# SSD groups 1 to 3: a chunk's turns behind the outputs and state of the chunk ahead of it, the last outputs two units later

## The reference

```python
proj = h @ w_in                       # split into z, xbc, dt_raw, sc_b, sc_c, sc_h, gates
xbc = silu(causal_dwconv(xbc, conv_w, conv_b))      # x heads, B and C of 4 groups
decay = exp(where(causal, a_cs[l] - a_cs[s], -inf)) # per head, in chunks of 128
y_diag = einsum((C B^T) * decay, x * dt)            # inside a chunk
state_c = einsum(B, decay_to_end, x * dt)           # h_new = h * d_c + state_c, chunk by chunk
y_off = einsum(C, state before the chunk, exp(a_cs))
y = (y_diag + y_off + d_skip * x) * silu(z)         # then a norm per group, then @ w_ssd_out
y_sc = (sc_b * causal_dwconv(sc_c * sc_h)) @ w_sc_out
```

## Time and profile before

| | |
|---|---|
| median of 3 runs | 1461.02 us (1460.84 to 1461.31) |
| the profiled execution | 1461.31 us |
| its span, first to last instruction | 1459.5 us |
| granted TensorE clock, mean | 1.000 |
| PE busy | 1451.3 us (99%) |
| PEld busy | 1196.2 us (82%) |
| DVE busy | 850.9 us (58%) |
| ACT busy | 518.7 us (36%) |
| POOL busy | 968.0 us (66%) |

### The profile page before, as it was taken

One profiled execution on the slowest core, in us unless ns is written; L12 is line 12 of the kernel. 1 busy time (PEld: TensorE's weight loads), 2 busy tenths in 40 slices (PEclk: granted clock), 3 DMA queues, 4 the chain that ended last, 5 costly groups with the idle time before them and its releaser, 6 DMA issues.

```text
span 1459.5 us, 22876 instructions
## 1 busy us (share of the span) xinstructions
PE 1451.3 (99%) x8038; PEld 1196.2 (82%) x8038; DVE 850.9 (58%) x1217; ACT 518.7 (36%) x931; POOL 968.0 (66%) x945
## 2 busy tenths in 40 slices
PE   9999999999999999999999999999999999999999
PEld 6788888888888888888988888888898888888887
DVE  3577796787688747423745545500258583846733
ACT  4481551362262311112522222200153554636441
POOL 5466767776766799888267777799426654655554
PEclk9999999999999999999999999999999999999999
DMA  9343433533533345435032232334223221222232
GB/s 378 119 128 114 161 102 130 178 110 124 185 112 121 119 137 171 139 104 200 15 101 90 97 101 96 100 121 144 87 98 116 78 82 59 86 72 72 72 130 73
DMA packets 68126, 172.31 MB, mean 118 GB/s; under 512 B 7744, under 2 KB 24512, under 8 KB 66656
## 3 DMA queue, kind: packets, MB, share of 16 engines
q1 hardware_dynamic: 45648, 150.57, 31.0%
q10 hardware_dynamic: 22416, 20.92, 4.7%
HBM read 167.20 MB, written 4.27 MB: 117 GB/s over the span
## 4 chain that ended last, share of the span: by engine, by line
PE 97%; DVE 1%; DMA 1%; ACT 0%; SPq 0%; issue 0%; DVEq 0%; ACTq 0%
PE ps L628 17%; PE ps L631 17%; PE ps L630 17%; PE ps L645 6%; PE ps L647 5%; PE ps L646 5%; PE ps L960 4%; PE ps L958 4%; PE ps L959 4%; PE ps L874 1%; PE ps L985 1%; PE ps L981 1%; PE ps L983 1%; PE ps L1155 1%; PE ps L1234 1%; PE ps L1235 1%
## 5 line engine op out<-in xcount | busy, mean ns | idle before, releaser
L578 POOL TENSOR_SCALAR w_hi<-raw 128x512 fp32r<-128x512 f32 x386 | 260.5, 693 | 462.7 <-PE ps L631 211.7
L583 POOL TENSOR_TENSOR w_lo<-raw,w_hi 128x512 fp32r<-128x512 f32 x386 | 543.6, 1429 | 0.0
L628 PE MATMUL ps<-h_hi,w_hi 128*128 128x512 f32 x880 | 344.5, 391 | 0.2
L631 PE MATMUL ps<-h_hi,w_lo 128*128 128x512 f32 x880 | 342.7, 389 | 0.0
L630 PE MATMUL ps<-h_lo,w_hi 128*128 128x512 f32 x880 | 342.5, 389 | 0.0
L628 PEld LDWEIGHTS ps<-h_hi,w_hi 128*128 128x128 f32 x880 | 165.2, 188 | 36.3 <-issue 2.4
L631 PEld LDWEIGHTS ps<-h_hi,w_lo 128*128 128x128 f32 x880 | 165.2, 188 | 34.9
L630 PEld LDWEIGHTS ps<-h_lo,w_hi 128*128 128x128 f32 x880 | 165.2, 188 | 33.7
L645 PE MATMUL ps<-h_hi,w_hi 128*128 128x512 f32 x352 | 140.2, 398 | 0.4 <-ACT qsq_hi L1653 0.4
L647 PE MATMUL ps<-h_hi,w_lo 128*128 128x512 f32 x352 | 137.4, 390 | 0.0
L646 PE MATMUL ps<-h_lo,w_hi 128*128 128x512 f32 x352 | 137.3, 390 | 0.0
(11 more groups left out here) (445 smaller groups left out, 2853.3 us busy)
## 6 DMA issues: line engine op xcount, KB each, us to landing
raw<-stream SPq DMA_DIRECT2D x231, 512.0 KB, 3.3
ada_raw<-ada SPq DMA_DIRECT2D x64, 256.0 KB, 3.3
ada<-ada_first SPq DMA_DIRECT2D x8, 1024.0 KB, 14.6
abc<-acs_dram ACTq DMA_DIRECT2D x16, 512.0 KB, 6.9
raw<-stream SPq DMA_DIRECT2D x8, 256.0 KB, 12.6
xr<-x_classes ACTq DMA_DIRECT2D x1, 2048.0 KB, 10.9
x_dram<-xr ACTq DMA_DIRECT2D x1, 2048.0 KB, 7.2
x_res<-x_dram ACTq DMA_DIRECT2D x2, 1024.0 KB, 7.7
```

What stands on the lines that cost most here:

```text
L578: nc.gpsimd.tensor_scalar(hi[:, w], raw[:, raw_slot, w], 1.0, 1.0, ALU.mult, ALU.mult).then_inc(split_hi, 1)
L583: ins = nc.gpsimd.tensor_tensor(lo[:, w], raw[:, raw_slot, w], hi[:, w].bitcast(F32), ALU.subtract)
L628: nc.tensor.matmul(ps[:, bank], hi[:, w], x_hi[:, k0 + k], start=start and k == 0, stop=False)
L631: mm = nc.tensor.matmul(ps[:, bank], lo[:, w], x_hi[:, k0 + k], start=False, stop=stop and k == tiles - 1)
```

## The change

For groups 1 to 3, PE's order behind `cover(2)` becomes: `cover(3)`, then for c = 0, 1, 2 `outputs(c)`, `state(c)`, `turn(c + 1)` with two covers behind each of the first two, then `sc(0)`, `sc(1)`, `outputs(3)`, `sc(2)` to `sc(5)`, `group_sums`. Before, a turn stood two chunks ahead: `turn(1)` behind `cover(2)`, `turn(2)` behind `state(0)`, `turn(3)` behind `state(1)`, with one cover between the blocks, and `outputs(3)` stood ahead of all six sc units. DVE's order follows: the y halves 5 to 7 are added ahead of `state(0)`, each chunk's `inputs` and `decayed` come behind the `state` of the chunk ahead, and the pieces 5 to 8 stand behind `state_input(1)` and `state_input(2)`. `decayed(3)` gets a wait for `inputs(3)`. Group 0 and ACT's order stay as they were.

```diff
--- before.py
+++ after.py
@@ -900,23 +900,38 @@
                 cover(1)
                 turn(0)
                 cover(2)
-                turn(1)
-                cover(3)
-                outputs(0)
-                state(0)
-                turn(2)
-                cover(4)
-                outputs(1)
-                state(1)
-                turn(3)
-                cover(5)
-                outputs(2)
-                state(2)
-                cover(6)
-                cover(7)
-                outputs(3)
-                for e in range(4 if first else 0, 6):
-                    sc(e)
+                if first:
+                    turn(1)
+                    cover(3)
+                    outputs(0)
+                    state(0)
+                    turn(2)
+                    cover(4)
+                    outputs(1)
+                    state(1)
+                    turn(3)
+                    cover(5)
+                    outputs(2)
+                    state(2)
+                    cover(6)
+                    cover(7)
+                    outputs(3)
+                    sc(4)
+                    sc(5)
+                else:
+                    cover(3)
+                    for c in range(NT - 1):
+                        outputs(c)
+                        state(c)
+                        turn(c + 1)
+                        if c < NT - 2:
+                            cover(4 + 2 * c)
+                            cover(5 + 2 * c)
+                    sc(0)
+                    sc(1)
+                    outputs(3)
+                    for e in range(2, 6):
+                        sc(e)
                 group_sums(g)
 
             group(0, True)
@@ -1950,6 +1965,8 @@
                     if c < NT - 1:
                         V.tensor_copy(dec_last[:, c], dec[:, c % 3, :, P - 1]).then_inc(chunk_steps, 1)
                         dve.wait_ge(chunk_steps, base + 5)
+                    else:
+                        dve.wait_ge(chunk_steps, base + 2)
                     TT(dec[:, c % 3], dec[:, c % 3], scm[:, c % 2].unsqueeze(1).broadcast_to([P, HEADS_G, P]),
                        ALU.mult).then_inc(chunk_steps, 1)
                     TT(abc[:, c % 3], abc[:, c % 3],
@@ -2070,25 +2087,24 @@
                     add_y_half(4)
                     decayed(0)
                     state_input(0)
-                    add_y_half(5)
+                    for n in (5, 6, 7):
+                        add_y_half(n)
+                    state(0)
                     inputs(1)
-                    add_y_half(6)
                     decayed(1)
-                    add_y_half(7)
-                    state(0)
+                    add_y(0)
                     state_input(1)
+                    ada_pieces(g - 1, (5, 6))
+                    state(1)
                     inputs(2)
                     decayed(2)
-                    add_y(0)
-                    state(1)
+                    add_y(1)
                     state_input(2)
+                    ada_pieces(g - 1, (7, 8))
+                    state(2)
                     inputs(3)
-                    add_y(1)
-                    ada_pieces(g - 1, (5, 6))
-                    state(2)
                     decayed(3)
                     add_y(2)
-                    ada_pieces(g - 1, (7, 8))
                     add_y(3)
                     gate()
                     ada_piece(g - 1, 9)
```

## The result

The changed kernel takes 1463.41 us (median of 20 runs, 1463.23 to 1465.67) against 1461.46 us for the kernel before beside it (20 runs, 1460.84 to 1462.01). The ratio is 1.0015 with a 95% interval of 1.0009 to 1.0021: a small loss. The profiled spans say the same: 1461.5 us against 1459.5, +2.0.

What follows compares the result with a forecast made beforehand. TensorE (PE) was taken as the bound, so only its waits could change. Per group, a 0.90 us loss at sc(4) less 0.33 gave +0.57; three groups made +1.7, from 1461.0 to 1462.7 us, range 1460.0 to 1467.2.

Steps and rivals of the forecast that it cites:

- Part 1: Turns moved behind outputs and state in groups 1 to 3: 0 to -0.1 us per group, taken as 0.
- The chunk set: DVE's state(1) through state_input(2), needed before PE's state(2): 9.5 us, not late by at least 1.5 us.
- The tail from T to `sc(4)`: T starts the dense matmuls behind outputs(3); scp ends T+11.76, sc(4) starts T+11.82 instead of 11.02, a 0.80 us wait.
- The choice of 1.22 and not 2.64 for the pieces: Two ada pieces between reduce and scp: 1.22 us undisturbed, as taken, against 2.64 us beside POOL's split.
- The first rival: POOL's split for sc(4) still runs when the reduce ends, slowing the pieces: +6.0 us, 1467.0 us; chance 0.24.
- The old 0.33: PE's loss per group at the start of sc(4) before the change, from POOL's late weight split; expected to go.
- `sc(5)` at 0: sc(5) needs short_out(0), expected done just before sc(5) is due: price 0, but 0.1 us from a wait.
- the other end, 0.5: Upper price at sc(5): +0.5 us, if POOL gets in front of DVE once more.
- What else moves: square_lo, SP's weight loads and a 0.5 us later DVE start in the next group: hidden or taken up by waits.
- the third: Rival: DVE's 9.5 us set runs late and PE waits at state(2) too; 1465.7 us at 1 us a group; chance 0.04.
- the fourth: Rival: PE gains at the turns and states, faster by over 2.9 us; chance 0.02.
- The second: Rival: tail quicker by 0.8 us or more, sc(4) does not wait: -1.0 us, 1460.0 us; chance 0.10.

Runs made afterwards that it cites:

- the last outputs alone: Kernel before with only outputs(3) moved behind sc(1) in groups 1 to 3, turns left in place: 1463.49 us, ratio 1.0016.
- The run with three pieces: Changed kernel with piece 12 moved ahead of short_conv(0), so three pieces instead of two stand between reduce and scp: 1466.05 us, ratio 1.0035.
- the run with the pieces behind `scp`: Changed kernel with pieces 10, 11 and 12 moved on DVE from around short_conv(0) to behind square_lo: 1463.51 us, ratio 1.0016.
- the run on the old 0.33: Kernel before with only pieces 13, 14 and 15 moved on DVE from ahead of short_conv(1) to behind it: 1462.48 us, ratio 1.001.

## Why the prediction came out as it did

The forecast of 1462.7 us was 0.7 under what was measured. Of this, 0.46 is the level: it was counted from 1461.0, the median of 3 runs, and the kernel before took 1461.46 beside the result. The rest is the difference to before: +1.7 expected, +1.95 between the medians, +2.07 in the groups of the trace. Its mechanism was right.

- **Part 1 at 0.** Right, and shown by the last outputs alone, which lose the whole of it; the new order's 0.03 to 0.04 us a group lie in the "0 to -0.1". The chunk set took 9.8 us, not 9.5, with 3.6 us to spare.
- **The tail from T to `sc(4)`.** Right to 0.01 us at each step: reduce T + 9.94, pieces 1.22, `scp` T + 11.76, PE T + 11.82. Taking group 0 for the coming order, and not the same engine's steps in group 2, is what made this exact. The run with three pieces shows that the wait is this sum: 0.62 more in, 0.61 more out.
- **The choice of 1.22 and not 2.64 for the pieces.** Right. The split was over 0.38 us before the reduce ended, where 0.37 was read from group 0. The first rival's condition did not come; the run with the pieces behind `scp` shows that its price is real, since a piece beside a split takes 1.78 us.
- **The old 0.33.** It did go, as `sc(4)`'s split came early. That it was the split is supported by PE's start following the split's end at three different latenesses. That DVE's two-input work made the split late is read from rows (3.42 us beside it, 2.55 beside the reduce); the one run that tried to take only this work away missed.
- **`sc(5)` at 0: the mis-sized term.** It was called 0.1 us from a wait, and it was closer. By the prediction's own numbers `short_out(0)` is done at 11.08 + 6.21 = T + 17.29 and the unit is due at T + 17.36; PE's step of 0.06 behind a DVE result, which the sum for `sc(4)` has, was left out here, and with it 0.01 us is left. So it came: `short_out(0)` ended at 375.71, about when the unit was due, PE came 0.05 later, and paid a restart of 0.11 us for a wait too short to appear in the table of waits. Three groups make 0.33 us, which is nearly all of the gap between +1.7 and +2.07. The run with three pieces, where `short_out(0)` has time to spare, has no such restart. A price of 0.1 was in reach, from the restart in the earlier trace rows; the other end, 0.5, was too high.
- **What else moves.** SP's weight loads were issued at about T + 5 and T + 12 (5 and 11 forecast) and hidden. The next group's first taps came later than the 0.5 us forecast, 1.3 us: 389.97, 8.15 behind the group's first matmul, against 387.77, 6.85 behind it, before. The wait for a piece's load took it up, as forecast: 3.29 us in the earlier trace rows, 2.02 after (DVE's timeline after).

```profile
389.97 0.67 DVE L1944 SCALAR_TENSOR_TENSOR cv<-ps,tab,cv 128x509 f32<-128x509 f32 x1
...
394.46 1.55 DVE L1888 CUSTOM_DVE_ANT_0 ada_raw<-ada_raw,c_row 128x512 f32<-128x512 f32 x1 [2.02 <-DMA ada_raw<-ada]
```

- **The other rivals.** No PE wait at `state(2)`, so the third is out; nothing gained at the turns, so the fourth is out. The second did not happen in this kernel, because no step of the tail was quicker. Its sum, about -1.0 us, is nearly what came when the pieces were moved out of the tail (0.28 to 0.30 a group, -0.9 us).

The Trainium skill (SBUF — State Buffer, Who interferes with whom) says that `tensor_reduce` never contends with GpSimd on trn2, while a VectorE instruction with two SBUF inputs contends with a GpSimd instruction that reads SBUF. The rows after agree: the reduce took 3.90 us with a split beside it, and the same half of the split took 2.55 us; beside a piece and `square_lo` in the run on the old 0.33 it took 3.42.

## What to carry to other kernels

Before moving an engine's block later, count what stands between its result and the next use of the buffer, in the queue of the engine that follows, and take the durations from a place of the same program that already has the coming order. Work that fills a gap (here the pieces) must move with the gap: DVE's waits shrank in the tail (ahead of the reduce from 3.55 to 1.37 us, ahead of `short_conv(1)` from 3.31 to none) and grew ahead of `add_y(3)` (from 5.14 to 7.22), and moving the pieces there removed the loss, while moving them later held weight loads on SP, and the loss came back elsewhere. A step that is "just in time" costs a restart even when its wait is too short to be listed, so price it.

## What the hardware showed that was not expected

A PE wait of 0.6 to 1.25 us left the granted clock at 1.00. The wait of 6.0 us was followed by 3.5 to 4.9 us at 0.50 in each of three groups, and that cost some 5.7 us, a third of the 18 us that the waits themselves cost. The Trainium skill (TensorE: Matmul & The Clock Gate, What's actually happening) says that the throttled clock is the default and that PE's activity releases it, and names 1.2 and 2.4 GHz as the two states; the stretches at 0.50 and 1.00 agree.

DVE's reduce took 3.68 us in the three places where PE stood idle beside it, and 3.88 to 3.91 in all 33 others of the nine traces, where PE worked; POOL's split stood beside it in both. The reason is open.

A load that waits for an engine on SP holds all loads behind it, weights included: 13 us without a weight load in one run, and a PE wait of 0.44 us at the unit whose weights were held.
